# A weight's high half times both input halves in one 512-column product

## What is computed

```python
def swiglu(x, w_gate, w_up, w_down):            # first block, ffn1 and ffn2
    return (jax.nn.silu(x @ w_gate) * (x @ w_up)) @ w_down
...
x = x + 0.5 * rmsnorm(h, ffn1_post_g[l])        # h = swiglu(...)
...
def sq_relu_mlp(h, w1, w2):                     # second block, each layer
    return jnp.square(jax.nn.relu(h @ w1)) @ w2
...
x = x + mx[5] * sq_relu_mlp(h2, w_ff1[l], w_ff2[l])
```

## Time and profile before

| | us |
|---|---|
| median of 3 runs (lowest to highest) | 2032.78 (2029.96 to 2034.72) |
| span of the profiled execution, first to last instruction | 2026.8 |
| PE busy | 1940.9 (96%) |
| PE weight load busy | 1721.4 (85%) |
| DVE busy | 1234.6 (61%) |
| ACT busy | 941.9 (46%) |
| POOL busy | 480.9 (24%) |

### The profile page before, as it was taken

How to read it: one execution, slowest core, us unless ns; L and a number is a source line. 1 busy time by engine, 2 the same in 40 slices (tenths; PEclk the granted TensorE clock), 3 DMA queues, 4 the chain that set the end, 5 groups by cost and what they waited for, 6 DMA issues and landing times.

```text
span 2026.8 us, 30560 instructions
## 1 busy us (share of the span) xinstructions
PE 1940.9 (96%) x12318; PEld 1721.4 (85%) x12318; DVE 1234.6 (61%) x1914; ACT 941.9 (46%) x1490; POOL 480.9 (24%) x326
## 2 busy tenths in 40 slices
PE   7999899899999999999799999999999899999999
PEld 6899887899997888787588788888877898799999
DVE  5688797779856863553763782354365947676410
ACT  5444447555456433334843541243255454765643
POOL 1201012000000000001444355455410000303887
PEclk9999999999999999999999999999999999999999
DMA  6987472566733112211023344466523233144554
GB/s 251 270 302 255 163 265 95 182 220 231 262 104 104 52 43 93 91 66 62 2 104 114 114 156 146 146 205 201 186 83 104 93 123 119 63 158 155 179 193 149
DMA packets 84637, 299.24 MB, mean 148 GB/s; under 512 B 9992, under 2 KB 13200, under 8 KB 84112
## 3 DMA queue, kind: packets, MB, share of 16 engines
q1 hardware_dynamic: 64512, 231.76, 33.3%
q0 software_dynamic: 17280, 60.95, 9.3%
q10 hardware_dynamic: 2704, 4.57, 0.6%
HBM read 296.18 MB, written 4.11 MB: 148 GB/s over the span
## 4 chain that ended last, share of the span: by engine, by line
PE 80%; DVE 9%; ACT 5%; DMA 3%; issue 2%; POOL 1%; ACTq 0%; DVEq 0%; POOLq 0%
PE ps L508 23%; PE ps L506 23%; PE ps L503 23%; DMA wr<-wstream 3%; DVE wl L436 3%; PE ps L1696 1%; ACT wh L420 1%; PE ps L1009 1%; PE ps L565 1%; PE ps L1011 1%; PE ps L1014 1%; ACT s L1144 1%; PE ps L1091 1%; DVE ST L1196 1%; DVE K L1785 1%
## 5 line engine op out<-in xcount | busy, mean ns | idle before, releaser
L503 PE MATMUL ps<-HH,wh 128*128 128x256 f32 (+1 forms) x2360 | 768.6, 326 | 19.9 <-ACT HH L1394 8.3
L508 PE MATMUL ps<-HH,wl 128*128 128x256 f32 (+1 forms) x2360 | 755.8, 320 | 6.6 <-DVE wl L436 5.6
L506 PE MATMUL ps<-HL,wh 128*128 128x256 f32 (+1 forms) x2360 | 754.6, 320 | 1.1 <-DVE HL L1408 1.0
L420 ACT ACTIVATE wh<-wr 128x1024 fp32r<-128x1024 f32 x440 | 461.5, 1053 | 381.4 <-PE ps L508 322.4
L503 PEld LDWEIGHTS ps<-HH,wh 128*128 128x128 f32 x2360 | 452.2, 192 | 61.5 <-issue 24.5
L436 DVE TENSOR_TENSOR wl<-wr,wh 128x1024 fp32r<-128x1024 f32 x297 | 361.0, 1223 | 217.3 <-ACT wh L420 215.2
L508 PEld LDWEIGHTS ps<-HH,wl 128*128 128x128 f32 x2360 | 452.0, 192 | 41.5 <-DVE wl L436 8.7
L506 PEld LDWEIGHTS ps<-HL,wh 128*128 128x128 f32 x2360 | 452.1, 192 | 35.8 <-issue 2.4
L436 POOL TENSOR_TENSOR wl<-wr,wh 128x1024 fp32r<-128x1024 f32 x143 | 345.8, 2423 | 199.6 <-ACT wh L420 198.8
L1246 POOL TENSOR_TENSOR s<-s,ST 128x512 f32<-128x512 f32 x56 | 57.3, 1039 | 737.5 <-DVE ST L1214 736.9
L508 PE MATMUL ps<-HIDH,wl 128*128 128x512 f32 (+1 forms) x512 | 173.1, 338 | 0.0
(11 more groups left out here) (251 smaller groups left out, 2558.2 us busy)
## 6 DMA issues: line engine op xcount, KB each, us to landing
wr<-wstream SPq DMA_DIRECT2D x440, 512.0 KB, 3.4
WM<-wmod POOLq DMA_DIRECT2D x68, 512.0 KB, 4.0
X<-wmod POOLq DMA_DIRECT2D x28, 512.0 KB, 6.3
NAB<-naskew POOLq DMA_DIRECT2D x16, 128.0 KB, 12.9
dilskew<-lines POOLq DMA_DIRECT2D x1, 2048.0 KB, 22.6
DILB<-dilskew POOLq DMA_DIRECT2D x2, 1024.0 KB, 12.1
COND<-cond ACTq DMA_DIRECT2D x2, 1024.0 KB, 4.6
CT<-consts POOLq DMA_DIRECT2D x1, 1216.0 KB, 9.5
```

Source lines behind the costliest of these rows:

```text
L420: ins = e.activation(self.WH[i % NSPL][:, :], self.WR[n % NRAW][:, :], ACT.Copy)
L503: e.matmul(out, wh, xh, start=i == 0, stop=False)
L506: e.matmul(out, wh, xl, start=False, stop=False)
L508: return e.matmul(out, wl, xh, start=False, stop=i == n_k - 1)
```

## The change

**The wide product.** In `three`, where the output is wider than the input half, one matmul multiplies the high weight by both input halves at once: `beside` makes an access pattern of two runs of 256 columns, the high half's and the low half's. The bank then holds in columns 0 to 255 high x high (and low x high, which is added there as before) and in columns 256 to 511 high x low. The two halves of the bank are added when it is emptied. HH and HL, NH and NL, HIDH and HIDL of layer 1 become parts of one tensor each, at the addresses that they had.

**Where.** In the down projections' pairs j = 0 to 2 (a tile now fills a bank, so a down projection takes seven banks instead of four); in layer 1's FF1 for f > 2; in layer 1's FF2 for d < 7. PE issues 10287 rows in place of 11007, 720 products fewer: 264, 232 and 224.

**The emptying.** Down projection: ACT copies columns 0 to 255 to Y, DVE adds columns 256 to 511 (L747 of the changed kernel), and the pair's square and gain read Y, not PSUM. FF1: ACT copies columns 0 to 255 to the second half of `tm` (`total`), DVE adds columns 256 to 511 to it and frees the bank, ACT's Relu reads `total`, and DVE's square multiplies `v` by `total`. The high and the low half of f are made after the copy and the add of tile f + 1. FF2: DVE adds the bank to X in two instructions.

```diff
+def beside(hi, lo):
+    return bass.AP(hi.tensor, hi.offset, [list(hi.ap[0]), [lo.offset - hi.offset, 2], list(hi.ap[-1])])
...
         for x in highs:
             w.wait_ge(*x)
+        if out.shape[-1] > xh.shape[-1]:
+            for x in lows:
+                w.wait_ge(*x)
+            e.matmul(out, wh, beside(xh, xl), start=i == 0, stop=False)
+            w.wait_ge(*self.low(n))
+            return e.matmul(out[:, 0:256], wl, xh, start=False, stop=i == n_k - 1)
...
+    def act_down(self, e, w, key, free):
...
+                self.make_high(e, w, *self.steps((key, j, h), ks))
+                if j < 3:
...
+                    w.wait_ge(*self.c("dense").at((key, j, h)))
+                    ins = e.activation(self.Y[:, 2 * j + h, :], self.main.item((key, j, h))[:, 0:256], ACT.Copy)
+                    ins.then_inc(*self.c("y_first").mark((key, j, h)))
+            if j < 3:
+                src, ready = self.Y[:, 2 * j:2 * j + 2, :].rearrange("p h t -> p (h t)"), self.c("y_sum").at((key, j, 1))
...
+    def dve_down(self, e, w, key, gain, free, side):
...
+                if j < 3:
+                    b = self.main.item((key, j, h))
+                    w.wait_ge(*self.c("y_first").at((key, j, h)))
+                    ins = e.tensor_tensor(self.Y[:, 2 * j + h, :], self.Y[:, 2 * j + h, :], b[:, 256:512], ALU.add)
+                    ins.then_inc(*self.c("y_sum").mark((key, j, h)))
...
+    def wide(key):
+        return key[0:2] == ("ff1", 1) and key[2] > 2 or key[0:2] == ("ff2", 1) and key[3] < 7
...
+            if self.wide(k):
+                x, m = self.X[:, d, 0:256], self.MOD[:, l, mod_i + d, 0:1]
+                ins = e.scalar_tensor_tensor(out=x, in0=self.main.item(k)[:, 256:512], scalar=m, in1=x,
+                                             op0=ALU.mult, op1=ALU.add)
...
     def act_ff(self, e, w, l, T):
...
+                if self.wide(key):
+                    e.activation(total, b[:, 0:256], ACT.Copy).then_inc(*self.c("f_first").mark(key))
+                    if self.wide(("ff1", l, f - 1)):
+                        high(f - 1, part)
+                    w.wait_ge(*self.c("f_sum").at(key))
+                    e.activation(v, total, ACT.Relu).then_inc(*self.c("relu").mark((l, f)))
...
     def dve_ff(self, e, w, l, T):
...
+                if self.wide(key):
+                    w.wait_ge(*self.c("f_first").at(key))
+                    e.tensor_tensor(total, total, b[:, 256:512], ALU.add).then_inc(*self.c("f_sum").mark(key))
+                    self.main.release(key, self.c("f_sum"), key)
+                    if self.wide(("ff1", l, f - 1)):
+                        low(f - 1, part)
+                    w.wait_ge(*self.c("relu").at((l, f)))
+                    w.wait_ge(*self.c("f_sum").at(key))
+                    e.tensor_tensor(v, v, total, ALU.mult).then_inc(*self.c("sqr").mark((l, f)))
```

More of the change, by code:

```diff
@@ L684, in dve_norm, with pe_down @@
         self.rm.release(key, self.c("n_v"), (key, 7))
+    def pe_down(self, e, w, key, name, rhs):
+        ks = range(22)
+        for j in range(4):
+            tiles = [(key, j, h) for h in range(2)] if j < 3 else [(key, j)]
+            for k in tiles:
+                self.main.take(k)
+                for x in self.main.before(k):
+                    w.wait_ge(*x)
+            for h in range(2):
+                b = self.main.item(tiles[h if j < 3 else 0])
+                c = 256 * j + 128 * h
+                self.dense(e, w, b[:, :] if j < 3 else b[:, 256 * h:256 * h + 256], (key, j, h), name, ks, [(c, c + 128)], rhs)
+            self.pe_squares(key, j)
@@ new lines, in act_down @@
+    def act_down(self, e, w, key, free):
+        ks = range(22)
+        self.table(e, "log_exp")
+        for j in range(4):
+            for h in range(2):
+                self.make_high(e, w, *self.steps((key, j, h), ks))
+                if j < 3:
+                    for x in free:
+                        w.wait_ge(*x)
+                    w.wait_ge(*self.c("dense").at((key, j, h)))
[3 more added lines that the diff above has]
+                src, ready = self.Y[:, 2 * j:2 * j + 2, :].rearrange("p h t -> p (h t)"), self.c("y_sum").at((key, j, 1))
+            else:
+                src, ready = self.main.item((key, j))[:, :], self.c("dense").at((key, j, 1))
+            self.act_square(e, w, key, j, src, [ready])
@@ L776, in pe_ffn, with act_ffn @@
             yield f
-        self.pe_pairs(e, w, ("down", n), (f"ffn{n}_w_down", 0), range(22), 4, self.hidden(n), True, False)
-    def act_ffn(self, e, w, n, free):
+        self.pe_down(e, w, ("down", n), (f"ffn{n}_w_down", 0), self.hidden(n))
+    def act_ffn(self, e, w, n, free, y_free):
         for f in range(22):
@@ L811, in dve_ffn @@
             yield f
-        self.dve_pairs(e, w, ("down", n), range(22), 4, lambda j: self.Y[:, 2 * j:2 * j + 2, :],
-                       f"ffn{n}_post_g", y_free, side)
+        self.dve_down(e, w, ("down", n), f"ffn{n}_post_g", y_free, side)
     def mod_steps(self, l):
@@ L2374, in act_ff, with high @@
         nf = 32 if l else 16
+        def high(f, part):
+            w.wait_ge(*self.c("dense").at(("ff2", l, 0, 7) if part else ("out", l, 0, 7)))
+            w.wait_ge(*self.c("sqr").at((l, f)))
+            ins = e.activation(self.hid(l)[0][:, f - nf * part, :], self.tm.item(("ff1", l, f))[:, 0:T], ACT.Copy)
+            ins.then_inc(*self.c("g_hi").mark((l, f)))
         for part in range(1 if l else 2):
```

80 lines of the change are left out of this document (56 added, 24 removed).

## The result

| | us |
|---|---|
| before, median of 4 runs (lowest to highest) | 2031.37 (2024.98 to 2034.72) |
| after, median of 4 runs | 2051.22 (2049.64 to 2053.05) |
| ratio after / before, 95% interval | 1.0101, 1.0088 to 1.0114 |
| span of the profiled execution after | 2050.4 |

The change makes the kernel 1.0% slower. Forecast were 2047.3 us and a loss of 14.5; it came to 19.9.

What follows compares the result with a forecast made beforehand. The prediction took PE, busy for 96% of a 2026.8 us span, as the bound. FF1 +15.6 and other stages -1.1 gave +14.5, a span of 2041.3; 6.0 more for the median gave 2047.3 us, range 2028.5 to 2053.

Steps and rivals of the forecast that it cites:

- What decided the sign: FF1: DVE's square, now from two SBUF inputs, must take turns with POOL like the low half; slower, chance 0.71.
- pairs of 7.15 us: FF1: DVE's square loses its turn to POOL every other tile, so two tiles take 7.15 us instead of 5.76.
- (a): Rival, FF1: low half and square both fit between two POOL ops each time; 2028.6 us, chance 0.17.
- (b): Rival, FF1: low half and square always go together and POOL waits, 2.90 us a tile; 2032.3 us, chance 0.11.
- (c): Rival, wide product: read from two places it costs two of 256 columns, so PE gains nothing; 2034 us, chance 0.02.
- PE saves 4.2 us: All changed stages: 720 fewer products save 3.1 us in FF1, 0.5 in FF2 and 0.6 in the down projections.
- The price of 233.3 ns for the arena's wide product: FF2 and down projections: a 512-column product costs 233.3 ns against two of 117.8, saving 2.3 ns each.
- Down projections, delay hidden: 0: First pair's end: the square's wait for the second add is hidden by 0.8 us; taken as 0.
- no new wait: Down projections: shorter by 0.3 us each, without any wait that was not there before.
- Six tiles pass before the turn bites, then 11 pairs at 1.39: FF1's 29 tiles: six at 2.77 us, one late block at 1.0, 11 pairs at +1.39; net +15.6 us.
- The slip: FF1: a tile wants 2.90 us against PE's 2.77, so DVE falls 0.13 us further behind POOL each tile.
- The clock stays at 1.00: FF1: PE's gaps of some 1.6 us a pair leave its clock at 1.00 (2.4 GHz); a fall would exceed the range.

Runs made afterwards that it cites:

- experiment 2: The changed kernel, but FF1's wide tile's square multiplies v by the PSUM bank, not total in SBUF, and frees the bank; 2030.94 us, 1.0005 of before.
- experiment 3: The changed kernel, but ACT squares v in place in FF1 and DVE has one op less a tile; 2030.58 us, 1.0003 of before.
- experiment 4: The kernel before, but in layer 1 DVE squares v by v, two SBUF inputs, instead of v by the bank; 2068.36 us, 1.0196 of before.
- experiment 6: The changed kernel, but DVE makes the weights' low halves of layer 1's FF1 and POOL begins with FF2; 2039.26 us, 1.0044 of before.
- experiment 10: experiment 6 with DVE's low half of the weights behind the tile's add instead of ahead of it; 2028.66 us, 0.9997 of before.
- experiment 5: The changed kernel, but FF1's wide product starts at f = 11 instead of f = 3, 21 wide tiles instead of 29; 2039.98 us.
- experiment 7: experiment 3 with the down projections as in the kernel before, so wide in FF1 and FF2 alone; 2026.93 us, 0.9984 of before.
- experiment 8: experiment 3 with the down projections' ACT square and DVE gain behind the next pair's first weight halves; 2028.62 us, 0.9989 of before.

## Why the prediction was right, and where it was not

**What decided the sign held.** The trace of before shows that an op from two SBUF inputs waits for POOL and that one that reads a bank doesn't; that the change turns the second kind into the first was read from the diff. Forecast were pairs of 7.15 us, POOL starts 2.5 and 4.6 apart and a square of over 2 us every second time; seen were 7.08, POOL ops in pairs of 4.91 after 2.16 idle, and squares of 2.6. Experiments 2, 3, 4, 6 and 10 take the conflict away or put it in alone. The Trainium skill (SBUF — State Buffer, section "Who interferes with whom") states the condition, two SBUF inputs against POOL, and all of them agree with it. Its "Issue order, not op shape, decides who blocks" also fits every turn read here from the kernel after and from experiment 5; the op of 4.89 us in the earlier trace rows stays unexplained.

**Rivals.** (a), all fits, is refuted by the waits of 18.4 us; (b), DVE keeps its turn at 2.90 a tile, describes experiment 5's six tiles, though at 2.83 us each and not 2.90, and nothing after them; (c), a wide product worth two of 256, is refuted by the steps of 347 to 353, where it wanted 360.

**Terms of the sum.**

- *PE saves 4.2 us.* Measured 2.9 to 5.5 over the stages. The split was off: FF2 0.5 forecast, 1.1 to 1.6 measured; FF1 3.1 forecast, 1.1 to 2.7 measured; down projections 0.6 forecast, 0.7 to 1.7 measured. The price of 233.3 ns for the arena's wide product, taken from layer 0's 512 columns, was too high: FF2's 1.6 us are 7 ns for each of 224, which leaves 228. By the Trainium skill's rule (TensorE: Matmul & The Clock Gate, section "Wait — 56ns, not 53.3ns?") the estimate would be 1.8 us for all; the traces give more.
- *Down projections, delay hidden: 0.* In the trace after that holds (PE 59.91 of 60.20). But "no new wait" was too much said: I looked at ACT's and DVE's durations at one pair's end, and not at DVE's side work, which waits for loads. In experiments 2, 3 and 5, whose program there is the change's, the stretch took 63.4 to 64.3, up to 2.5 us more than undisturbed. That the profiled execution of the change has none of this is luck.
- *Six tiles pass before the turn bites, then 11 pairs at 1.39.* This step failed, by some 3 us. With the saving taken out, the forecast has 15.6 + 3.1 = 18.7 us of stalls. Measured, as the length of a stalled step less 347 ns, are twelve stalls of 1.3 to 1.5 us in FF1, 17.4 in all, and two, of 1.5 and 2.4, at FF2's start: 21.3 us, one for each of the 14 pairs of the 29 tiles. The bite comes with the first wide tiles. The slip itself is real (experiment 5: six tiles, at half the forecast slip), but it starts from a POOL with 0.48 us to spare. In the change it doesn't: when POOL takes over from DVE, its first three ops run without a gap, so POOL's next op already waits when DVE wants its second turn (1862.77, 2.63 us). The trace of before showed that as well:

```profile
1853.25 7.50 POOL L436 TENSOR_TENSOR wl<-wr,wh 128x1024 fp32r<-128x1024 f32 x3 [81.67 <-ACT wh L420]
```

I took POOL's steady rows for the whole stage and didn't look at its start.
- *The clock stays at 1.00.* It did through FF1's twelve gaps of 1.1 to 1.3 us (PEclk 1.00 in 1860 to 1950). At FF2's start it stood at 0.51, which is 1.2 GHz, for 3.4 us, less than a microsecond behind a gap of 2.00 us: some 1.6 us lost, as its steps of 640 ns replace steps of 347. The prediction had looked for such a fall in FF1 only, and had FF2 start as before.

Together, against the first trace of before: 21.3 + 1.6, less a saving of 1.9 in FF1 and 1.5 in FF2, is 19.5; the two stages show 19.4. The down projections take off 1.2, so the four stages show 18.2, and the medians 19.9; 2 us of median are what these comparisons can't tell. Of the 3.7 us between 18.2 and the forecast of 14.5, the stalls are some 2.6 and the clock 1.6, and the saving, 4.6 against 4.2, gives 0.4 back. The mechanism and the sign were right, the size came out low, and the measured time lies in the upper part of the range. The forecast stood on a median of 2032.8; before measured 2031.4 with one run more.

**The gain without the turns.** With the conflict gone, PE's stream is 3 to 5.5 us shorter in the traces, 0.15 to 0.3%, and the ratios to before lie between 0.9984 and 1.0008. Experiments 7 and 8 are the only ones whose interval lies below 1; it ends 0.0004 and 0.0002 short of it, and that of the unchanged program lies above 1 as narrowly. That a version of this change beats the kernel before is likely, and isn't shown. The medians point to 7 (square on ACT, wide in FF1 and FF2, down projections left alone), the stage lengths to 8, with 305.0 us against 307.0.

## What to carry to other kernels

When an edit changes where an operand lies, PSUM or SBUF, ask which engines that op can now run beside: here one DVE input moved from a bank to SBUF cost 37 us by itself (experiment 4), and a program with 720 products fewer got slower. Check a steady pattern at its first cycles too, since who is waiting when a stage starts decides who goes first later; and when work moves between two engines that feed each other, sum the ring and not the loads. A saving of 0.2% needs an unchanged kernel timed beside it.

## What the runs showed of the hardware

- **A passed turn.** In the kernel after, a DVE op that waits for POOL goes in as POOL's op ends, even with POOL's next op ready; the DVE op right behind it doesn't (2.17, then 2.61 us). The op of 4.89 us at 1154.88 is the one seen that was passed over. Some 0.05 us decide it (experiment 5): a square issued 0.02 us ahead of POOL's start took 0.41, one issued 0.03 after it 2.65.
- **What a turn costs.** Two POOL ops with a 256-column DVE op between them took 4.91 to 4.94 us, against 4.75 back to back: 0.16 to 0.19, where 0.22 was estimated.
- **The clock.** PE's gap of 2.00 us before the low products at FF2's start was followed by 1.2 GHz in the kernel after, and not in experiment 5, in which the gap there is as long (PE idle for 2.0 of the 5 us):

```profile
1949.00:1954.00 5.00, 3.01 (x17) 2.27 (x16) 0.00 (x0) 2.33 (x3) 4.42 (x2) 1.00 0.22 58
```

The gap alone doesn't decide it. The two traces of before have eight stretches of 3.4 us at 1.2 GHz each, and the second has one more, in a part of the kernel that the change doesn't touch:

```profile
1001.10:1011.40 10.30, 9.04 (x46) 7.09 (x46) 3.25 (x6) 6.44 (x11) 0.00 (x0) 0.50 0.00 0
```

Half of PE's 9.04 busy us, about 4.5, is an estimate of what that one costs, and the two spans differ by 4.6.
